# Gate vectors of a modulated block through DRAM rows instead of products with the identity

## The reference

```python
def modulate(x, g, shift, scale):
    return rmsnorm(x, g) * (1 + scale) + shift

for i in range(DEPTH):
    mod = jax.nn.silu(c) @ ada_w[i] + ada_b[i]
    sh1, sc1, g1, sh2, sc2, g2 = jnp.split(mod[:, None, :], 6, axis=-1)
    mod_c = jax.nn.silu(c_ctx) @ ada_w[i] + ada_b[i]
    csh1, csc1, cg1, csh2, csc2, cg2 = jnp.split(mod_c, 6)
    h = modulate(x, norm_mix_g[i], sh1, sc1)
    hc = modulate(ctx, norm_mix_g[i], csh1, csc1)
    ...
    x = x + g1 * y
    x = x + g2 * swiglu(modulate(x, norm_ffn_g[i], sh2, sc2), ...)
    if not last:
        ctx = ctx + cg1 * yc
        ctx = ctx + cg2 * swiglu(modulate(ctx, norm_ffn_g[i], csh2, csc2), ...)
```

## Time and profile before

| | us |
|---|---|
| median of 3 runs (2597.03 to 2598.75) | 2597.41 |
| time of the profiled execution | 2599.55 |
| its span, first to last instruction | 2597.7 |
| TensorE busy | 2537.9 |
| VectorE busy | 1427.0 |
| ScalarE busy | 532.9 |
| POOL busy | 316.6 |

### The profile page before, as it was taken

How to read it: one execution, slowest core, us unless ns; L and a number is a source line. 1 busy time by engine, 2 the same in 40 slices (tenths; PEclk the granted TensorE clock), 3 DMA queues, 4 the chain that set the end, 5 groups by cost and what they waited for, 6 DMA issues and landing times.

```text
span 2597.7 us, 38620 instructions
## 1 busy us (share of the span) xinstructions
PE 2537.9 (98%) x16192; PEld 1971.3 (76%) x16192; DVE 1427.0 (55%) x2632; ACT 532.9 (21%) x1249; POOL 316.6 (12%) x367
## 2 busy tenths in 40 slices
PE   8999999999999999999999999999998999999998
PEld 7888886864788898687467757888886656666997
DVE  1575454865247544483345825555434378863775
ACT  1342220100134122011012921000002143321000
POOL 2001112210100111131000000000000145510110
PEclk9999999999999999999999999999999999999999
DMA  7331114987533211488642012322222534434552
GB/s 264 114 126 55 51 50 147 307 283 248 169 119 122 73 35 51 160 279 294 241 157 81 2 33 81 98 82 74 89 85 69 146 114 127 130 97 146 171 171 105
DMA packets 252563, 340.76 MB, mean 131 GB/s; under 512 B 7236, under 2 KB 178372, under 8 KB 252264
## 3 DMA queue, kind: packets, MB, share of 16 engines
q1 hardware_dynamic: 240592, 310.66, 36.1%
q10 hardware_dynamic: 8920, 17.67, 2.2%
q0 software_dynamic: 2880, 9.96, 1.1%
HBM read 337.08 MB, written 1.19 MB: 130 GB/s over the span
## 4 chain that ended last, share of the span: by engine, by line
PE 93%; DVE 2%; DMA 2%; issue 1%; ACT 1%; POOL 0%; ACTq 0%; SPq 0%; POOLq 0%; DVEq 0%
PE PS L1000 17%; PE PS L397 13%; PE PS L443 10%; PE PS L669 7%; PE PS L1255 6%; PE PS L1042 5%; PE PS L783 5%; PE PS L979 4%; PE PS L682 3%; PE PS L1088 2%; PE PS L1232 2%; PE PS L435 2%; PE PS L749 1%; PE PS L407 1%; PE PS L558 1%
## 5 line engine op out<-in xcount | busy, mean ns | idle before, releaser
L1000 PE MATMUL PS<-MEM 128*128 128x256 f32 (+1 forms) x2632 | 447.5, 332 | 0.7 <-DVE MEM L2399 0.7
L1000 PEld LDWEIGHTS PS<-MEM 128*128 128x128 f32 x2632 | 406.8, 190 | 41.0 <-DVE MEM L2399 0.9
L397 PE MATMUL PS<-MEM 128*128 128x256 f32 x1632 | 358.2, 381 | 5.7 <-DMA MEM<-w_up 5.7
L1358 ACT ACTIVATE MEM<-PS 128x256 f32<-128x256 f32 (+4 forms) x405 | 167.4, 428 | 927.0 <-PE PS L397 229.1
L397 PEld LDWEIGHTS PS<-MEM 128*128 128x128 f32 x1632 | 309.9, 191 | 49.2 <-DMA MEM<-w_up 6.5
L443 PE MATMUL PS<-MEM 128*128 128x512 f32 x608 | 263.4, 594 | 5.9 <-POOL MEM L2879 2.8
L1961 DVE SCALAR_TENSOR_TENSOR MEM<-MEM 128x512 f32<-128x512 f32 x280 | 217.8, 811 | 61.8 <-DMA MEM<-ada_w 55.9
L443 PEld LDWEIGHTS PS<-MEM 128*128 128x128 f32 x608 | 114.9, 190 | 150.5 <-issue 140.5
L2829 POOL TENSOR_TENSOR MEM<-MEM 128x1 f32<-128x1 f32 (+1 forms) x34 | 21.8, 643 | 1271.7 <-DVE MEM L1907 815.2
L669 PE MATMUL PS<-MEM 128*128 128x256 f32 x768 | 172.3, 382 | 0.0
L1255 PE MATMUL PS<-MEM 128*128 128x512 f32 (+1 forms) x512 | 170.6, 486 | 0.0
(11 more groups left out here) (377 smaller groups left out, 3268.2 us busy)
## 6 DMA issues: line engine op xcount, KB each, us to landing
MEM<-w_in SPq DMA_DIRECT2D x54, 1024.0 KB, 5.2
MEM<-ada_w SPq DMA_DIRECT2D x48, 1024.0 KB, 7.3
MEM<-w_up SPq DMA_DIRECT2D x32, 1024.0 KB, 5.4
MEM<-w_down SPq DMA_DIRECT2D x32, 1024.0 KB, 5.1
MEM<-ssm_w_in SPq DMA_DIRECT2D x24, 1024.0 KB, 5.4
MEM<-ffn_gate SPq DMA_DIRECT2D x22, 1024.0 KB, 5.2
MEM<-ffn_up SPq DMA_DIRECT2D x22, 1024.0 KB, 5.1
MEM<-ffn_down SPq DMA_DIRECT2D x20, 1024.0 KB, 5.0
```

Source lines behind the costliest of these rows:

```text
L397: ins = pe.matmul(bank[:, 0:T], W[:, k, c * P:(c + 1) * P], XT[:, k, :], start=k == 0, stop=k == KT - 1)
L1000: ins = pe.matmul(out, left[:, k, :], right[:, k, :], start=k == 0, stop=k == 3)
L1358: act.activation(out, view(b), func, **kw).then_inc(S("bank_read_by_act"), 1)
```

## The change

The gates no longer go through TensorE. The bias is now added in row form: VectorE reads the bank `("modrow", first)`, adds `BROW` (the bias in the same row form, loaded by POOL in each layer of the first block) and writes `AROW`, which now has two parts (one for each group of a layer). TensorE transposes `AROW` as before, and `ada_outs` becomes a plain copy. ScalarE stores each stream's gate from `AROW` to DRAM in two transfers (`gates_stored`), and POOL loads it back broadcast to all 128 partitions (`gates_loaded`). `gate_rows`, its banks and its copies are dropped, and so are the products in `gate_by_tile`. `PV2` loses its 96 bias columns, which moves what lies behind it. At the end of the first block, ScalarE's squares of tile 1 stand ahead of the copy of the first V bank.

```diff
+GATES = ((0, 2, 2), (0, 5, 2), (1, 2, 1), (1, 5, 1))
...
-        AROW = mem(256, at=part + 9216)
+        AROW = mem(2, 256, at=R2B + 33280)
+        BROW = mem(2, 256, at=R2B + 33792)
...
     def ada_products(n):
-                bank = take(("modrow", first), "act")
+                bank = take(("modrow", first), "dve")
...
     def ada_turned(n):
-                    ins = pe.transpose(bank[:, j * P:(j + 1) * P], AROW[:, j * P:(j + 1) * P], ident)
+                    ins = pe.transpose(bank[:, j * P:(j + 1) * P], AROW[:, first % 24 // 18, j * P:(j + 1) * P], ident)
...
-            def gate_rows(n, l, which, streams):
-
-                pe.wait_ge(S("mods_ready" if l else "gains_ready"), 1)
-                for t in range(streams):
-                    for half in range(2):
-                        bank = take(("gr", n, t, half), "act")
-                        for k in range(4):
-                            g = MODF[:, l, t, which, 4 * half + k:4 * half + k + 1].to_broadcast([P, P])
-                            ins = pe.matmul(bank[:, k * P:(k + 1) * P], g, ident, start=True, stop=True)
-                        done(ins)
...
                 if t == 0:
-                    gate_rows(0, 0, 2, 2)
                     turn_normed(0, (0,))
...
-            gate_rows(2, 1, 2, 1)
+            pe.wait_ge(S("mods_ready"), 1)
...
@@ scalar @@
+            def gates_stored(n):
+
+                l, which, streams = GATES[n]
+                part = which // 5
+                emptied(act, ("modrow", 24 * l + 18 * part))
+                k = 2 * which - 9 * part
                 for t in range(streams):
+                    for e in range(2):
+                        row = 32 * (2 * e + t) + k
+                        act.dma_start(io["gate_dram"][n, t].rearrange("(a e n) -> e a n", a=2, e=2)[e], AROW[row:row + 2, part, :])\
+                           .then_inc(S(f"gates_stored{n}"), 16)
...
-                copy(("modrow", first), AROW, lambda b: b[:, 0:256])
+                gates_stored(2 * l)
                 if l == DEPTH - 1:
                     act.wait_ge(S("x_gained"), NT * (2 * l + 2))
                     modulated(0, (1,))
                     squares2(0, (0,))
-                    peek(act, ("mod", first))
-                    copy(("modrow", first + 18), AROW, lambda b: b[:, 0:256])
...
+            squares2(0, (1,))
             copy(("v2", 2), VV[:, 2, :], lambda b: b[:, 0:T])
-            squares2(0, (1,))
             copy(("v2", 3), VV[:, 3, :], lambda b: b[:, 0:T])
-            gate_rows(0, 2)
             modulated(0, (0,))
             for t in range(NT):
                 copy(("v2", t), VV[:, t, :], lambda b: b[:, 0:T])
+            gates_stored(3)
...
@@ vector @@
+            def ada_rows(first):
+
+                l, part = first // 24, first % 24 // 18
+                dve.wait_ge(S("ada_rows_loaded"), 16 * (l + 1))
+                b = filled(dve, "dve", ("modrow", first))
+                read(dve.tensor_tensor(AROW[:, part, :], b[:, 0:256], BROW[:, part, :], ALU.add))
...
-                            ins = dve.tensor_tensor(MOD[:, l, t, cols], b[:, q:q + k], PV2[:, bias], ALU.add)
+                            ins = dve.tensor_copy(MOD[:, l, t, cols], b[:, q:q + k])
...
                     residual("dn", l, 0, t)
                     stats(t, 0)
+                ada_rows(24 * l)
                 if l == DEPTH - 1:
                     modulated(0, (1,))
-                peek(dve, ("modrow", 24 * l))
                 ada_sums(ADA_DOWN)
...
                             ada_outs(ADA_UP + ADA_DOWN)
+                            ada_rows(24 * l + 18)
...
             rms_scaled(0, 1)
             ada_outs(ADA_UP + ADA_DOWN)
+            ada_rows(24 * (DEPTH - 1) + 18)
             ada_outs(ADA_DOWN)
...
-                            emptied(dve, ("gr", n, tiles // NT - 1, 1))
+                            dve.wait_ge(S(f"gates_loaded{n}"), 16 * GATES[n][2])
...
@@ gpsimd @@
                 rows(2 * l + 2)
+                pool.dma_start(BROW[:, :, :], io["ada_rows"][l]).then_inc(S("ada_rows_loaded"), 16)
...
+            def gates_loaded(n):
+
+                pool.wait_ge(S(f"gates_stored{n}"), 32 * GATES[n][2])
+                if n:
+                    pool.wait_ge(S("x_tiled"), max(v for (m, _), v in tiled_at.items() if m == n))
+                for t in range(GATES[n][2]):
+                    pool.dma_start(GR[:, t, :], io["gate_dram"][n, t].partition_broadcast(P)).then_inc(S(f"gates_loaded{n}"), 16)
+
             for n in range(3):
                 for t in RMS_TILES[n][0 if n else NT:]:
                     power(MS2[:, t:t + 1])
+                gates_loaded(n)
```

More of the change, by code:

```diff
@@ L79 @@
 ADA_UP, ADA_DOWN = 12, 6
-W_AB, W_GM, W_GF, W_C, W_CW, W_CB, W_NG, W_D, W_SK, W_DTB, W_AL = 0, 96, 112, 128, 144, 240, 272, 288, 304, 320, 321
-NPV2 = 322
+W_GM, W_GF, W_C, W_CW, W_CB, W_NG, W_D, W_SK, W_DTB, W_AL = 0, 16, 32, 48, 144, 176, 192, 208, 224, 225
+NPV2 = 226
+GATES = ((0, 2, 2), (0, 5, 2), (1, 2, 1), (1, 5, 1))
 def lam_init(l):
@@ L1103, in gate_by_tile @@
                 later = normed_banks(1)
-                rows = [take(("gr", 3, 0, half), "act") for half in range(2)]
                 W = a_slab(io["ffn_gate"][l], 0)
@@ L1117, in gate_by_tile @@
                 turn_normed_tile(3, 1, later)
[L1118 to L1122, removed]
                 for half in range(2):
@@ L1424, in _ @@
                         act.dma_start(CST[:, C_MSK:NCST], io["cst"][:, C_MSK:NCST]).then_inc(S("tables_loaded"), 16)
-                    if l and t == 0:
-                        emptied(act, ("mod", 24 * (l - 1)))
-                        copy(("modrow", 24 * (l - 1) + 18), AROW, lambda b: b[:, 0:256])
                     for s in range(1 + t):
                         copy(("u", l, s, t), UTK[:, t, 256 * s:256 * s + 256], lambda b: b[:, 0:256])
+                if l:
+                    gates_stored(1)
                 if l == 0:
@@ L1583, in _ @@
                     copy(("up", l, f), HID[:, f, :], lambda b: b[:, 0:T], ACT.Relu)
-                first = 24 * l
                 if l == DEPTH - 1:
@@ L1978, in ada_outs @@
                             cols = slice(o, o + 4 * (k - 1) + 1, 4)
-                            bias = slice(W_AB + 48 * l + o, W_AB + 48 * l + o + 4 * (k - 1) + 1, 4)
                             q = P * j + 32 * (2 * e + t)
-                            ins = dve.tensor_tensor(MOD[:, l, t, cols], b[:, q:q + k], PV2[:, bias], ALU.add)
+                            ins = dve.tensor_copy(MOD[:, l, t, cols], b[:, q:q + k])
                 read(ins)
@@ L2043, in _ @@
                     read(dve.tensor_scalar(YA[:, g, :], b[:, 0:T], pv(V_PS + g), None, ALU.mult))
+                if l:
+                    for n in range(2):
+                        dve.wait_ge(S(f"gates_stored{n}"), 32 * GATES[n][2])
                 dve.memset(ZT[:, :, 0:1], 0.0)
@@ L2429, in feed_forward_sevens @@
                 if l == 0:
+                    for m in range(2, 4):
+                        dve.wait_ge(S(f"gates_stored{m}"), 32 * GATES[m][2])
                     modulated(n, (1,))
@@ L2504, in narrow_joined @@
                         settle()
-                        emptied(dve, ("gr", n, 0, 1))
+                        dve.wait_ge(S(f"gates_loaded{n}"), 16 * GATES[n][2])
                         b = filled(dve, "dve", ("n", 2, half))
@@ L2576, in down_joined @@
                         settle()
-                        emptied(dve, ("gr", n, 1, 1))
+                        dve.wait_ge(S(f"gates_loaded{n}"), 16 * GATES[n][2])
                         link(scaled(DA1, 0, ca))
@@ L2935, in _ @@
                 power(MS2[:, t:t + 1])
+            gates_loaded(3)
             pool.dma_start(GR[:, 1, :], io["final_g"].partition_broadcast(P)).then_inc(S("gain_loaded"), 16)
@@ L3056 @@
     cos, sin, rot = rope_tables()
+    ada_rows = np.zeros((DEPTH, P, 2, 256), np.float32)
+    for l in range(DEPTH):
+        for k in range(12):
+            for e in range(2):
+                for t in range(2):
+                    ada_rows[l, 32 * (2 * e + t) + k % 9, k // 9] = a["ada_b_2"][l, 512 * k + 256 * e:512 * k + 256 * e + 256]
     arrays = {
-        "pv2": pv2, "ctx": a["ctx_2"], "ada_w": a["ada_w_2"], "w_qkv": a["attn_w_qkv_2"][0], "w_o": a["attn_w_o_2"][0],
+        "pv2": pv2, "ada_rows": ada_rows, "ctx": a["ctx_2"], "ada_w": a["ada_w_2"], "w_qkv": a["attn_w_qkv_2"][0], "w_o": a["attn_w_o_2"][0],
         "ssm_w_in": a["ssm_w_in_2"][0], "ssm_w_out": a["ssm_w_out_2"][0], "ffn_gate": a["ffn_w_gate_2"], "ffn_up": a["ffn_w_up_2"],
```

10 lines of the change are left out of this document (2 added, 8 removed).

## The result

The kernel after the change takes 2612.48 us (median of 4 runs, 2610.96 to 2614.52) against 2597.92 us (4 runs) before: a ratio of 1.0056, 95% interval 1.0044 to 1.0068. It is slower by 14.6 us. The forecast was 2607.5 us, +10.1, in a range that ended at 2612.0. The sign and the large term came true; the size did not, and the time lies half a microsecond above the range.

The account below looks back on a forecast made before the run. TensorE, busy 98% of the span, was taken as the bound wherever nothing else ends later. Terms 4.3 + 2.3 + 1.8 - 0.3 + 1.8 + 0.2 = +10.1 on a median of 2597.41 gave 2607.5 us, range 2603 to 2612.

Parts of the forecast that it names:

- The sign: Whole kernel: the change makes it slower, chance 0.91, against 0.06 for same and 0.03 for faster.
- the large term: End of first block: TensorE waits for VectorE's late addition of the last modulation rows, +4.3 us.
- Gate products: Four places on TensorE: removing them takes 3.57 us off the path in the first, gains 0 in the others.
- The hand-over, +4.3: End of first block: TensorE restarts 7.85 us late behind VectorE's addition; net +4.3 us, the 3.57 saved already subtracted.
- The clock after it, +2.3: V products after the first block's 8.4 us idle: a lowered clock slows them, +2.3 us, range 1.3 to 3.1.
- Bias rows loaded in the first block, +1.8: Waits for w_up in both layers: POOL's new load lengthens them and makes a clock fall likelier; bounds 0 and 3.2.
- The transfer part, 0.7 us for each layer: Waits for w_up: nothing hides the 0.25 MB transfer, 0.7 us in each layer, 1.4 in all.
- the 0.4 for a fall of the clock behind the second wait: Second layer of the first block: longer waits for w_up make a clock fall likelier, 0.4 us added.
- VectorE at the first layer's rows, +0.2: First layer: a 0.43 us addition ahead of the running sums delays freeing ring slots for w_down, 0 to 0.4 us.
- The second place, +1.8 with bounds 0 and 2.6: Second gate-product place (n=1): idle grows from 0.72 to 4.3 us and very probably lowers the clock, +1.8 us.
- Third and fourth place: Last two gate-product places: third already cold, -0.3 us (bounds -1.2, +0.4); fourth has short idles, 0 (up to 1.8).
- Stores and loads of the gates, 0: ScalarE's twelve stores and POOL's six loads: issued in idle time or needed much later, cost 0.

Follow-up runs that it names:

- e2: Changed kernel with VectorE's small outputs and last-row addition moved ahead of the last tile's scaling: 2602.26 us, ratio 1.0015 to the kernel before.
- r2: The changed kernel run and profiled a second time, without an edit, one execution: 2614.41 us.
- e5: Kernel before with only the 0.25 MB bias-row load added in each layer, its data read by nobody: 2601.34 us, ratio 1.0009.
- e3: Changed kernel with VectorE's addition for the first layer's first rows moved behind the running sums: 2609.19 us, ratio 1.0045 to the kernel before.
- e4: Changed kernel with 16 useless identity products ahead of the last tile's transposes in the second place: 2607.62 us, ratio 1.0038 to the kernel before.
- r1: The kernel before profiled a second time, without an edit: 2601.13 us with its profile, 2597.54 us beside it.
- e9: Kernel before with 24 useless identity products ahead of the transposes in its third place, nothing else: 2595.77 us, ratio 0.9987.
- e1: Changed kernel with POOL's bias-row load issued later, behind the waits for w_up: 2608.89 us, ratio 1.0039 to the kernel before.
- e6: Changed kernel with the edits of e1, e2 and e3 together: 2598.99 us, ratio 1.0005 to the kernel before.
- e7: e6 plus the 16 useless products of e4 in the second place: 2595.80 us, ratio 0.9990 to the kernel before.
- e8: e7 plus 32 useless products ahead of the transposes in the third place: 2591.52 us, ratio 0.9977 to the kernel before.

## Why the prediction was wrong in size and right in kind

**Gate products: right.** 3.57 us in the first place alone. e2, where nothing takes them away again, shows -3.05 over that stretch.

**The hand-over, +4.3: right.** The restart came 7.6 us late (1346.29, against 1332.82 and a lag of 5.9 by then), forecast 7.85; the addition took 0.41 us, forecast 0.43. The forecast put all twelve small outputs (0.93 us) ahead of the addition; only eight (0.66 us) stand there, which is the difference. **The clock after it, +2.3: in its range** (whose bounds 1.3 and 3.1 the prediction doesn't work out), near the lower end: the V products lost 8.35 - 7.09 = 1.3 and the transposes behind them none. L508 itself took 0.25 more. 7.6 + 0.25 + 1.3 - 3.6 = 5.6, against 6.6. In r2 the V products lost 2.6 and the whole was 6.95. e2 shows the cause by taking the wait away.

**Bias rows loaded in the first block, +1.8: too small, and the step that failed.** The transfer part, 0.7 us for each layer, was right: +0.65 and +0.66 in e5, +0.99 and +0.60 in after. What failed is the 0.4 for a fall of the clock behind the second wait. It cost after 16.72 - 64 x 7.07 / 32 = 2.6 us and e5 3.0. I had weighted it low because the one profile of before had passed 2.94 us of waiting at full clock. One profile did not tell enough, as all of them together show. The loss is how much longer than 90.05 us, their time at full clock, the 416 records behind the second wait take (it differs by up to 0.1 us from the figures read from shorter groups above):

| | 0.25 MB load at these waits: after, r2, e2, e3, e4, e5 | no load at these waits: before, r1, e9, e1, e6, e7, e8 |
|---|---|---|
| first wait for w_up | 3.76, 4.16, 3.35, 3.66, 3.40, 3.42; mean 3.6 | 2.77, 2.66, 2.70, 2.77, 2.85, 2.60, 3.52; mean 2.8 |
| second wait | 3.54, 3.71, 3.70, 3.40, 3.58, 3.60; mean 3.6 | 2.94, 3.51, 2.72, 2.85, 2.96, 2.79, 2.87; mean 2.9 |
| loss behind the second | 2.6, 1.7, 1.7, 1.7, 2.8, 3.0; mean 2.3 | 0, 1.6, 0, 1.7, 0, 0, 1.7; mean 0.7 |

With the load the clock fell behind the second wait in six of six, without it in three of seven. The waits cost 0.8 + 0.6 us more and the clock 1.6 more, where 0.4 was forecast: together 3.0 us against 1.8, within its bounds of 0 and 3.2. The lags from 440 to 1140 us give the same, a mean of 4.2 with the load and 1.2 without. The 5.7 of the first column is more than that, because before's profile happened to be one without a loss and after's one with a large one. Timed alone (e5) the load is 2.3 us, between 0.3 and 4.7, which does not rule out the 1.8.

**VectorE at the first layer's rows, +0.2: not shown.** The w_down waits cost 1.2 us more than in the earlier trace rows, but e3 keeps a wait of 0.9 us without the addition ahead, r1 has one of 1.05, and r2, with the addition, has 0.54.

**The second place, +1.8 with bounds 0 and 2.6: the other term that was mis-sized.** By the lags it is 2.7 in after, e1 and e3, 3.3 in e6, and 3.7 in r2 and e2: above the upper bound in all of them. I read its price from the third place, from the evictions there (1.7) and "up to 0.9" for the next products. The rows show 0.8 on the transposes and 2.0 on the products behind them, which are wide and follow while the clock is still low; in the third place they come at the end of the low stretch. e4 shows the cause: with the clock held the whole term is gone. The Trainium skill (TensorE: Matmul & The Clock Gate, Terms) prices a throttled stretch at its length times the share of pulses withheld. The clock rows put the low stretch from about 1581.4 (0.86 in the 2 us from 1580) to 1588.3, which by that rule would be an estimate of 3.4; after shows 2.7. TensorE idles for 1.14 us within the stretch, and idle time loses nothing to the clock.

**Third and fourth place: right**, -0.3 and nothing to be seen. **Stores and loads of the gates, 0: right**; no wait of TensorE names them.

**The reference execution.** Spans give +12.7 and the medians +14.6. The profiled execution of before was 1.6 us above its own median and that of after 0.2 below: 12.7 + 1.6 + 0.2. On one chip 21 executions of the kernel before lay between 2595.4 and 2602.9. The forecast stood on a median of 2597.41 for before, which a fourth execution moved to 2597.92; this alone is as large as the half microsecond by which the time lies above the range. The range had been cut at +14.6 where the upper bounds add up to +16.0.

**What the terms add up to now.** The hand-over with its clock (5.6 to 7.0), the second place (2.7 to 3.7), the third (-0.3) and the load (3.0) come to 11.0 to 13.4 us, against +10.1 forecast and +14.6 measured, whose interval is +11.4 to +17.7. By the timed runs, from after, e1 takes 3.7 us, e2 10.3 and e4 4.9. Together 18.9; e7, which has them all and e3, lies 16.7 below after, which agrees as far as these intervals can tell.

**What stays open.** Why the clock falls behind one wait of 2.9 us and not behind another, and why the waits for w_down and for the second w_up differ by up to 1 us between executions of the same program, was not settled. So the load's share is known only to some 2 us. The difference between e1 and after, 3.7 us (4.4 by the ratios), is hardly larger than that between e3 and after, 3.4 us (2.9 by the ratios), though e3 takes away one wait of 0.65 us at most; both are about the half-width of after's interval (3.1 us).

## What to carry to other kernels

When an operation on the way between two engines is given to a third one, look at what stands ahead of it in that engine's order: a 0.4 us addition behind one tile's work cost 5.6 us, and moved forward it gave 3. A product that is off the path may still hold the clock: before dropping it, look at how long TensorE is idle then, and price at half the clock all that runs next while the clock is low, also the products behind the first ones. Profile the kernel before twice where a few microseconds matter: one profile can miss a loss that another execution of the same program has.

## What the runs showed of the hardware

- Useless products in an idle stretch paid: 3.2 us by e7 against e6, 4.3 by e8 against e7, 3.1 by e9 against before. In the traces the filled place itself gives 3.2, 2.2 and 2.5 of these. In e4, e8 and e9 they left 0.73, 0.90 and 0.89 us of idle in the place, and what came next ran at full rate.
- The clock after a wait is no function of that wait's length alone: full after 2.94 us, low after 2.85 us (e1). After an idle time of 2.45 us behind the same work it was low in before and full in e5.
- A load of 0.25 MB from POOL's queue, issued ahead of a wanted slab that SyncE had issued, lengthened that wait by about its own transfer time, 0.65 us in e5 and 0.6 to 0.8 in the mean of all profiles, against 0.7; 0.75 MB by 1.3 to 2.1 us. Single executions differ by as much: e8, with the load moved away, waited 3.52 us at the first place. The Trainium skill (Trainium Kernel Development and Optimization, Key Constraints) says that these queues share the 16 DMA engines, and the waits agree.
